# Float32 matmuls for three of four frame blocks: one up pass ahead for the last block, two blocks down dense, two sparse

## What is computed

```python
def block(args):
    xk, ek, gk = args                       # 128 frames; 128 expert numbers and gates per frame
    a = jnp.einsum('nd,ned->ne', xk, u_emb[ek])
    coef = jax.nn.gelu(a, approximate=False) * gk
    return jnp.einsum('ne,ned->nd', coef, v_emb[ek])
```

## Time and profile before

| | |
|---|---|
| median of 3 runs | 1831.16 us (1828.79 to 1844.94) |
| span of the profiled execution | 1734.2 us |
| PE busy | 1694.7 us, 98% |
| DVE busy | 1105.1 us, 64% |
| ACT busy | 577.1 us, 33% |
| POOL busy | 927.0 us, 53% |
| DMA | 351.04 MB, mean 202 GB/s |
| granted TensorE clock | 0.998 |

### The profile page before, as it was taken

The page is one execution under the profiler, slowest core; times in us unless marked ns, Lnnn a source line. Parts: engine busy times, 40 slices in busy tenths (PEclk is TensorE's granted clock), DMA queues, the critical chain, the costliest instruction groups (busy, mean ns, idle before and its releaser), DMA issues.

```text
span 1734.2 us, 23540 instructions
## 1 busy us (share of the span) xinstructions
PE 1694.7 (98%) x7845; PEld 1396.2 (81%) x7845; DVE 1105.1 (64%) x2968; ACT 577.1 (33%) x929; POOL 927.0 (53%) x859
## 2 busy tenths in 40 slices
PE   7999999989999999999999999999999999999997
PEld 6877877778888878888888888888888888888886
DVE  4249968445788864444444444444688888888886
ACT  4333225343322322222222222223333333333333
POOL 3644400003354007777777777771777777777710
PEclk9999999999999999999999999999999999999999
DMA  5322231126667645444447544555999999999991
GB/s 162 105 61 58 65 65 55 42 73 219 214 236 255 218 134 145 146 145 145 145 144 244 146 146 146 146 146 165 385 390 376 370 375 361 373 375 362 378 331 49
DMA packets 182674, 351.04 MB, mean 202 GB/s; under 512 B 35600, under 2 KB 118928, under 8 KB 182448
## 3 DMA queue, kind: packets, MB, share of 16 engines
q1 hardware_dynamic: 147776, 282.74, 49.2%
q0 software_dynamic: 34816, 67.41, 10.8%
HBM read 289.04 MB, written 61.02 MB: 202 GB/s over the span
## 4 chain that ended last, share of the span: by engine, by line
PE 63%; DVE 0%; issue 0%; DVEq 0%; ACT 0%
PE psum L404 21%; PE psum L403 21%; PE psum L405 21%; DVE mixed L2095 0%; DVE mixed L2072 0%; DVEq L2019 0%; DVE rstd_final L815 0%; DVE rstd_final L821 0%; DVE rstd_final L817 0%; DVE rstd_final L819 0%; DVE rstd_final L813 0%; ACT rstd_final L2206 0%; DVE rstd_final L2081 0%; DVE rstd_final L2079 0%
## 5 line engine op out<-in xcount | busy, mean ns | idle before, releaser
L2281 POOL DMA_INDIRECT gate_map<-gate_total,gate_at x384 | 403.5, 1051 | 203.8 <-DVE same_expert L2026 113.2
L403 PE MATMUL psum<-x_hi,ts_hi_u 128*128 128x512 f32 x1024 | 399.1, 390 | 4.0 <-PEq L1641 2.3
L404 PE MATMUL psum<-x_lo,ts_hi_u 128*128 128x512 f32 x1024 | 398.4, 389 | 0.0
L405 PE MATMUL psum<-x_hi,ts_lo_u 128*128 128x512 f32 x1024 | 398.4, 389 | 0.0
L1529 DVE TENSOR_TENSOR ts_lo_u<-ts_raw_u,ts_hi_u 128x1024 fp32r<-128x1024 f32 x116 | 142.3, 1226 | 339.5 <-ACT ts_hi_u L1524 336.8
L403 PE MATMUL psum<-v_hi,c_hi 128*128 128x512 f32 x768 | 298.8, 389 | 0.0
L404 PE MATMUL psum<-v_lo,c_hi 128*128 128x512 f32 x768 | 298.8, 389 | 0.0
L405 PE MATMUL psum<-v_hi,c_lo 128*128 128x512 f32 x768 | 298.8, 389 | 0.0
L1560 ACT ACTIVATE ut_out_u<-psum 128x512 f32<-128x512 f32 x128 | 76.5, 598 | 494.1 <-PE psum L405 494.1
L2186 ACT ACTIVATE v_hi<-v_raw 128x1024 fp32r<-128x1024 f32 x128 | 135.8, 1061 | 312.4 <-PE psum L405 312.4
L2269 POOL DMA_INDIRECT sparse_rows<-in_peer_v,v_row x128 | 164.8, 1288 | 123.2 <-DVE sparse_more L2062 34.5
(11 more groups left out here) (251 smaller groups left out, 2307.5 us busy)
## 6 DMA issues: line engine op xcount, KB each, us to landing
ts_raw_u<-in_peer_u SPq DMA_DIRECT2D x128, 512.0 KB
v_raw<-in_peer_v SPq DMA_DIRECT2D x128, 512.0 KB, 6.1
gate_map<-zeros SPq DMA_DIRECT2D x32, 768.0 KB, 6.5
up_acts<-ut_out_u SPq DMA_DIRECT2D x128, 192.0 KB, 1.9
act_in<-up_acts SPq DMA_DIRECT2D x128, 192.0 KB, 6.3
gate_in<-gate_map SPq DMA_DIRECT2D x128, 192.0 KB, 6.8
raw_in<-in_w_in SPq DMA_DIRECT2D x56, 256.0 KB, 2.8
ts_raw_wq<-in_peer_wq SPq DMA_DIRECT2D x16, 512.0 KB, 6.6
```

Source lines behind the costliest of these rows:

```text
L403: nc.tensor.matmul(out, l_hi, r_hi, start=first, stop=False)
L404: nc.tensor.matmul(out, l_hi, r_lo, start=False, stop=False)
L405: return nc.tensor.matmul(out, l_lo, r_hi, start=False, stop=last)
L2281: nc.gpsimd.indirect_dma_start(gate_cells, bass.IndirectOffsetOnAxis(places["gate_at"][:, b, j:j + 1], 0), dn.total[:, b, j:j + 1], None). ...
```

## The change

Only two blocks remain dense (`DENSE_BLOCKS = NB - 2`). Block 3 becomes the *early* block and block 2 the *late* one; both are summed slot by slot (`SparseSum`).

- **Early pass.** When `route` has ended, PE multiplies the other 104 up tiles with block 3 alone, in plain float32 without a split: 26 groups of 4 tiles, with x of the block (`early_x`, `x_hi` plus `x_lo`, added by DVE at the end of `route`) as the weights and 512 columns of tiles as the moving side, 8 matmuls a group. SP loads 2 MB a group in a ring of three; ACT takes the gelu, SP stores to `up_acts_early`.
- **Up.** The 104 tiles are then done by three passes with 384 columns (`UP_FRAMES`) instead of 512.
- **Rows of the early block.** POOL first scatters the gates of blocks 0 and 1 (256), with no wait for up tiles between them, and then gathers rows and activations for block 3. DVE adds 96 of the rows beside up tiles 40 to 103 of `experts` (`FIRST_ADD`, `UP_ADDS`) and the other 32 beside down tiles 0 to 19 (`LEFT_BY`).
- **Down.** `product` writes `coef` (128 x 256) and PE multiplies it with v in plain float32, 4 matmuls a tile. The splits of v and coef are gone. v is loaded in pairs of tiles into a ring of 20, of which 12 lie in the space of the early tiles and 8 in that of `x_hi` and `x_lo`, which comes free after up. Gate and activation lie beside each other in one map and are loaded as one (`map_in`). Up to four coefficients lead.
- **Rows of the late block.** Gathers for block 2 start once up is done and those of block 3 are through. DVE adds the 128 rows beside down tiles 26 to 123 (`FIRST_LATE`, `late_by`).
- **End.** Block 3 is finished in down, at tiles 20 to 22, block 2 behind the last additions.

The core of the diff:

```diff
-DENSE_BLOCKS = NB - 1
+DENSE_BLOCKS = NB - 2
+LATE_BLOCK, EARLY_BLOCK = NB - 2, NB - 1
+UP_FRAMES = FRAMES - P
+GROUP = 4
+GROUPS = (NKEYS - ROUTE_TILES) // GROUP
...
+class EarlyTiles:
+    RING = 3
...
+    def product(self, nc, pe, g):
...
+        if g >= 2:
+            pe.wait_ge(self.bank_read, g - 1)
+        pe.wait_ge(self.loaded[g % self.RING], 16 * (g // self.RING + 1))
+        for k in range(KT):
+            last = nc.tensor.matmul(self.bank[g % 2], self.x[:, k], self.tiles(g)[:, :, k], start=k == 0, stop=k == KT - 1)
+        last.then_inc(self.product_done, 1)
...
+            dve.wait_ge(wq.product_done, SETS)
+            nc.vector.tensor_tensor(early.x[:], x_hi[:, :, UP_FRAMES:FRAMES].bitcast(F32), x_lo[:, :, UP_FRAMES:FRAMES].bitcast(F32),
+                                    ALU.add).then_inc(early.x_done, 1)
...
+class SparseSum:
+    RING = 8
+    BODY = 8
...
+    def gather_row(self, nc, pool, places, v_rows, j):
+        r = j % self.RING
+        if j >= self.RING:
+            pool.wait_ge(self.row_added, j - self.RING + 1)
...
+    FIRST_ADD, UP_ADDS = 40, 96
+    LEFT_BY = 20
+    FIRST_LATE = 26
...
+    def early_by(n):
+        return max(0, n - FIRST_ADD) * UP_ADDS // (TILES - FIRST_ADD)
+    def early_left_by(e):
+        return UP_ADDS + min(SLOTS - UP_ADDS, e * (SLOTS - UP_ADDS) // LEFT_BY)
+    def late_by(e):
+        return min(SLOTS, max(0, e - FIRST_LATE) * SLOTS // (NKEYS - FIRST_LATE - LAST))
...
+                if e >= COEFS:
+                    dve.wait_ge(down_done, e - COEFS + 1)
+                nc.vector.tensor_tensor(dn.coef[:, e % COEFS], dn.map_in[:, i, 0], dn.map_in[:, i, 1], ALU.mult).then_inc(coef_done, 1)
...
+            soon.zero_more(nc, dve)
+            for m in range(DENSE_BLOCKS * SLOTS):
+                total_gate(m, *place(m))
             for n in range(TILES):
                 if n + 2 < TILES:
                     ut.split_lo(nc.vector, dve, n + (R + 2))
-                for m in range(n * PER_TILE, min((n + 1) * PER_TILE, DENSE_BLOCKS * SLOTS)):
-                    total_gate(m, *place(m))
-            for e in range(EARLY):
+                for j in range(early_by(n), early_by(n + 1)):
+                    soon.add_row(nc, dve, acc, gates, j)
+            for e in range(COEFS):
                 product(e)
...
+            for e in range(NKEYS):
+                if e >= COEFS:
+                    product(e)
+                for j in range(early_left_by(e), early_left_by(e + 1)):
+                    soon.add_row(nc, dve, acc, gates, j)
...
+                for j in range(late_by(e), late_by(e + 1)):
+                    late.add_row(nc, dve, acc, gates, j)
...
+                return nc.tensor.matmul(psum[:, n, :], dn.coef[:, e % COEFS, b * P:(b + 1) * P],
+                                        dn.v(e)[:, half * 512:half * 512 + 512], start=first, stop=final)
...
+            def gather_all(some, cells):
+                for j in range(some.BODY):
+                    some.gather_act(nc, places, cells, j)
+                for j in range(some.RING // 2, some.RING):
+                    some.gather_row(nc, pool, places, v_rows, j)
+                for j in range(some.BODY, 2 * some.BODY):
+                    some.gather_act(nc, places, cells, j)
+                for j in range(some.RING, SLOTS):
+                    some.gather_row(nc, pool, places, v_rows, j)
+                    if j + some.BODY < SLOTS:
+                        some.gather_act(nc, places, cells, j + some.BODY)
             pool.wait_ge(zeroed, 16 * ZERO_STORES)
             for m in range(DENSE_BLOCKS * SLOTS):
-                if m % PER_TILE == 0:
-                    pool.wait_ge(ut.product_done, R + m // PER_TILE)
...
+            gather_all(soon, early_d)
             pool.wait_ge(ut.product_done, NKEYS)
...
+            gather_all(late, late_cells)
```

More of the change, by code:

```diff
@@ L1577, in route @@
+def route(c, x_hi, x_lo, places, expert, gates, zeroed, wq, ut, early, before_start, nc, io, sem, sb, psum, ident, iota, map_d, late_d, early_d, **_):
     G = 4
@@ L1669, in _ @@
                     store_zeros(x)
+            sp.wait_ge(wq.product_done, SETS)
+            for g in range(2):
+                early.load(sp, io["peer_u"], g)
             for t in range(sel_up, ROUTE_TILES):
@@ L2134, in _, with down_bank @@
         def _(pe):
-            def down_bank(i, n, first, final):
+            def down_bank(e, n, first, final):
                 b, half = divmod(n, 2)
-                cols, dcols = slice(b * P, (b + 1) * P), slice(half * 512, half * 512 + 512)
-                return three_pass(nc, psum[:, n, :], dn.c_hi[:, i, cols], dn.c_lo[:, i, cols],
-                                  dn.v_hi[:, i, dcols], dn.v_lo[:, i, dcols], first, final)
-            def down(e, i, first):
-                pe.wait_ge(c_lo_done, e + 1)
+                return nc.tensor.matmul(psum[:, n, :], dn.coef[:, e % COEFS, b * P:(b + 1) * P],
+                                        dn.v(e)[:, half * 512:half * 512 + 512], start=first, stop=final)
@@ L2144, in down, with wait_tile @@
+            def wait_tile(e):
+                if e % 2 == 0:
+                    pe.wait_ge(v_in[e % V_RING // 2], 16 * (e // V_RING + 1))
+                pe.wait_ge(coef_done, e + 1)
+            def down(e):
+                wait_tile(e)
                 for n in range(OUTS):
-                    last = down_bank(i, n, first, False)
+                    last = down_bank(e, n, e == 0, False)
                 last.then_inc(down_done, 1)
             def last_tiles(b):
-                for i in range(RING):
+                for e in range(NKEYS - LAST, NKEYS):
@@ L2151, in last_tiles @@
                     if b == 0:
-                        pe.wait_ge(c_lo_done, NKEYS - RING + i + 1)
+                        wait_tile(e)
                     for n in (2 * b, 2 * b + 1):
-                        last = down_bank(i, n, False, i == RING - 1)
-                        if i == RING - 1:
+                        last = down_bank(e, n, False, e == NKEYS - 1)
+                        if e == NKEYS - 1:
                             last.then_inc(bank_done, 1)
+            for g in range(GROUPS):
+                early.product(nc, pe, g)
@@ L2158, in _ @@
+            up_hi, up_lo = x_hi[:, :, 0:UP_FRAMES], x_lo[:, :, 0:UP_FRAMES]
             with pe.Fori(0, TILES // 2) as it:
                 for par in range(2):
-                    ut.product(nc, pe, x_hi, x_lo, it * 2 + (R + par), par, False)
-            for i in range(RING):
-                down(i, i, i == 0)
-            with pe.Fori(1, NKEYS // RING - 1) as it:
-                for i in range(RING):
-                    down(it * RING + i, i, False)
+                    ut.product(nc, pe, up_hi, up_lo, it * 2 + (R + par), par, False, ut.bank[par][:, 0:UP_FRAMES])
@@ L2166, in _ @@
+            for e in range(NKEYS - LAST):
+                down(e)
             for b in range(DENSE_BLOCKS):
@@ L2202, in _ @@
                     act.wait_ge(acc_done, 2 * n + half + 1)
-                    nc.scalar.activation(dn.rows[:, n, dcols], acc[:, b, dcols], ACT.Square,
+                    nc.scalar.activation(dn.early_rows[:, n, dcols], acc[:, b, dcols], ACT.Square,
                                          accum_out=ss[:, b, half:half + 1]).then_inc(squared, 1)
```

409 lines of the change are left out of this document (227 added, 182 removed).

## The result

| | before | after |
|---|---|---|
| median of 4 runs | 1830.39 us (1828.79 to 1844.94) | 2061.65 us (2057.53 to 2064.09) |
| ratio after / before | | 1.1242, 95% interval 1.1194 to 1.1291 |
| span of the profiled execution | 1734.2 us | 2055.7 us |

The change makes the kernel 12% slower. The sign is as forecast, the size is not: 1867 us were predicted, with 1905 as the upper end. The four runs of the kernel after took 1.8 us more than their spans; the median of the kernel before stands 96 us above the one span that was profiled.

The account below looks back on a forecast made before the run. PE was taken as the present bound, POOL and DMA second. PE alone gave −37.9 us (1696 us), but POOL's chain of gathers made the span 1769.6 us; with the 97.0 us gap 1867 us, range 1797 to 1905.

Parts of the forecast that it names:

- 97 us: Whole run: gap between profiled span 1734.2 and median 1831.2 us, added unchanged to the forecast span to give 1867 us.
- the forecast's sum: Whole span: POOL's chain of scatters and gathers ends late, giving 1769.6 against 1734.2 us, +35.4 us.
- Rival (d): Early pass or later: scatters wait for landing, or gathers and v loads saturate the DMA; span above 1820 us, chance 0.10.
- pitch of a row in the up stage: Up stage: POOL's time for one row and one activation gather of block 3, taken as 3.1 us.
- pitch of a late row: Down stage: POOL's time for one row and one activation gather, taken as 2.95 us.
- zero of 0 to 2: Barrier at 636 us: block 3's address arithmetic and x_hi plus x_lo on DVE cost 0 to 2 us, summed as 0.
- half a hold per instruction: POOL's gathers: each 1.28 us DVE addition holds one POOL instruction 0.64 us on average, less 0.12 us.
- the sign that I had named: Up stage from tile 40: PE below 100% and `ts_lo_u` late behind `early_rows` would show the forecast right.
- POOL's chain of rows: Up into down: block 3's rows 8 to 95 at 3.1 us let down start at 1289 instead of 1248 us.
- POOL without idle time except issue: From 640 us to the last gather: POOL never idles except its 0.30 us issue gaps, a sign the forecast is right.
- rival (b): A draw, including the DMA as bound in down (449 against PE's 439 us): span 1716 to 1752 us, chance 0.20.
- The Trainium skill's rule that I had weighed: SBUF: two-input DVE instructions and GpSimd instructions reading SBUF exclude each other; the second waits, 1.34 against 0.96 us in the trace.

Follow-up runs that it names:

- c4: Kernel after with POOL waiting once for all 256 gate totals, then scattering without waits; on a disturbed chip, 2102.1 us.
- g1: Kernel after, unedited, run again on a quiet chip: 1771.92 us, span 1770.1, beside a kernel before of 1741.2 us.
- e7: Kernel after without the early pass's plain loads after its third group: span 2054.3 us, beside a kernel before of 1834.04 us.
- e8: Kernel after with scatters paced by PE's products, and without block 2's 128 activation gathers: span 1843.3 us, beside a kernel before of 1834.04 us.
- e5: Kernel after with POOL waiting for DVE's gate totals once per 16 scatters instead of before each: span 2046.2 us.
- c1: Kernel after, unedited, run again on a disturbed chip: 2071.5 us, beside a kernel before of 1845.25 us.
- c3: Kernel after with scatters paced, 5 per early group then 3 per up tile, on a disturbed chip: 1893.9 us.
- the paced one: Kernel after with scatters waiting for PE's products, 5 per early group, then 3 per up tile: 1786.0 us quiet, 1893.9 us disturbed.
- c2: Kernel before, unedited, run again with its own trace on a disturbed chip: 1857.7 us.

## Why the prediction was right and wrong

**The step that failed** is the sentence "The profiled span and the median of the runs lie 97.0 us apart (1831.2 − 1734.2), which I leave as they are: 1867 us." I treated 97 us as something fixed around the span. In every run that had both numbers, device time and span differ by 1.8 to 2.2 us. The 97 us were late increments in the up stage, of the kind that c4 ties to POOL's stream, and the change makes that stream denser and takes its pace away. In the kernel before POOL waits for the up tile's product ahead of every fourth scatter, so a delay of that very increment stops POOL too; in the changed kernel nothing in POOL's scatters waits for PE, and they go on past the gaps (256 in 358 us, against 343 in g1). Cost: from about 97 to 286 us (2055.7 − 1770.1). With the 97 us carried over as a constant, 1867 us could not hold it. That the median is slower, as forecast, is mostly luck: of its 231 us about 31 are those of the forecast's sum (1771.9 − 1741.2 in g1), the rest is a loss that the forecast did not have. Rival (d), "worse", got 0.10 and a mechanism about bandwidth and landing, which is not what happened; e7 excludes it for the early pass.

**The sum itself came out** where it could be seen alone, in g1, but not for its reasons in the up stage:

| step | forecast | g1 |
|---|---|---|
| early pass | 178.3 us | 178.2 |
| last scatter issued | 977 us | 986.6 |
| row 8 of block 3 | 1010 us | 1020.0 |
| pitch of a row in the up stage | 3.1 us | 2.85 (rows 8 to 96) |
| down starts | 1289 us | 1283.3 |
| pitch of a late row | 2.95 us | 2.96 (rows 8 to 112) |
| last gather | 1737 us | 1733.1 |
| end of the last matmul | 1760 us | 1761.0 |
| span | 1769.6 us | 1770.1 |

The close end hides errors that cancel. The scatters were 10 us late: they began at 643.8 us, not 640, and the first 48 took 1.37 us each beside DVE's totals, which I had priced at 1.26. PE left the barrier at 640.4 us, not 636.5: 2.9 us waiting for the sum of `x_hi` and `x_lo`, which I had put at zero of 0 to 2:

```profile
PEld psum L1623 <- DVE early_x L1982: 2.9, 1, 2.9
```

The rows of the up stage went the other way, 22 us better: from row 40 on they come 2.77 us apart, exactly PE's 1.5 per 4.16 us, with POOL issuing without idle time. My average of half a hold per instruction was too dear; why, no run here separates. And from 1098 us to the end of the stage PE never stood:

```profile
1100.00:1250.00 150.00, 150.00 (x867) 150.00 (x866) 110.00 (x97) 52.15 (x73) 116.87 (x109) 1.00 1.00 365
```

So the sign that I had named, PE below 100% from tile 40 on and `ts_lo_u` late behind `early_rows`, is there only at the first rows: PE loses about 11 us near 1010 us, where DVE waits 12.2 us for the first activations (forecast: 5 to 8). The start of down was to be the end of POOL's chain of rows; it was the end of PE's own work, 433 us and 32 us of stops. That 1283 lies near 1289 is luck.

Missed altogether were the other 19 or so of these 32 us: halfway through the up stage SP issues six loads of 1 MB for v, and the loads of the coming up tiles stand behind them. SP's issues in g1 in that stretch and after it:

```profile
1061.03 3.04 SPq L1534 DMA_DIRECT2D ts_raw_u<-in_peer_u  x1
...
1083.51 0.41 SPq L1534 DMA_DIRECT2D ts_raw_u<-in_peer_u  x1
```

PE stops four times between 1054.9 and 1083.6 us, 14.8 us in all from start to start, and its matmuls stand 0.32 us apart instead of 0.17 for a while behind them; in the kernel after 1328.6 to 1339.5 us is the same place. It moved the start of down but hardly the end: POOL, whose stream sets the end, waited for additions only 3.1 us in all.

**"POOL without idle time except issue"** from the first scatter to the last gather is confirmed by g1. What ended waits in its down stage (us, times, longest):

```profile
DVE coef L2172 <- DMA map_in<-gate_act_map: 61.5, 26, 5.4
DVE mixed L2098 <- DMA late_rows<-in_peer_v,v_row: 54.4, 36, 2.5
...
POOL late_rows L2070 <- issue: 39.0, 128, 0.3
POOL late_act L2075 <- issue: 39.0, 128, 0.3
```

In down PE does wait for `coef`, and POOL's chain gave the end. But POOL is not the only bound there. In e8 half of its instructions of the stage were gone; window and waits of e8:

```profile
1450.00:1800.00 350.00, 343.68 (x793) 149.33 (x794) 197.51 (x255) 1.54 (x5) 141.03 (x121) 1.00 1.02 405
...
DVE coef L2177 <- DMA map_in<-gate_act_map: 152.6, 69, 5.0
POOL late_rows L2070 <- DVE late_more L2103: 107.2, 39, 17.9
```

POOL now waits for additions and DVE for the maps, at 405 GB/s and a share of 1.02, and down still took 474 us, not the 439 to 450 that I had expected. The total mixes two parts. Tiles 0 to 25, ahead of the late rows, took 116 us against 107 in the three kernels beside it on that chip (e5 to e7); from tile 26 on e8 took 358 us, those three 367 to 369, g1 369, and PE alone would take 350. So POOL's missing instructions were worth about 10 of 19 us, and about 8 remain. These I put down to the DMA, rival (b), by the waits and the 405 GB/s; no run takes DMA traffic away there. Disturbed chips disturb down as well (483, 486 and 492 us in c1, c4 and c3), so that e8 can be held only against its neighbours. The Trainium skill's rule that I had weighed ("SBUF — State Buffer", section "Who interferes with whom") stays supported by the 1.37 us beside the totals.

**In what sense slower.** On a quiet chip the change costs 1771.9 / 1741.2, 1.8% in single runs, as the spans of the forecast said (1769.6 / 1734.2, 2.0%); on a disturbed one 12.3% (2071.5 / 1845.3), the median 12.4%. It is slower on both. No version here beats the kernel before: the paced one is 2.7% slower on a quiet chip and 2.6% on a disturbed one (1893.9 / 1845.3; 1.9% against the 1857.7 us of c2), where it takes back 178 us of the change's 226.

**Not shown.** Whether short pauses of POOL are enough or its wait for PE's own increment is needed, which I only argue (the paced early pass took 183.5 us in c3 and 180 in e8); what the pace alone is worth in the kernel before on a disturbed chip; and whether scatters do more harm than gathers: both do some, as 1404 us in the kernel after shows for gathers. Since each chip was used in one group of runs only, its state at that time cannot be told from the chip itself. Why one does it and another not, and why 44.80 us, I cannot say.

## What to carry to other kernels

Before a sum is made against a profile, put its span beside the times: where they differ by more than a few us, something happens in the timed runs that this profile doesn't show, and it has to be found and priced, not carried along. Compare kernels, and above all experiments, only with the kernel before from the same chip; four clean runs on a quiet chip could decide nothing here and led to a wrong theory all the same. A wait that looks redundant because it is nearly always met may be what stops an engine in time; if POOL's indirect DMAs are to be set free of the product's pace, look at a profile from a chip where increments come late.

## What the runs showed of the hardware

- On two of the five chips of the experiments, while POOL issues indirect DMAs one behind the other (0.96 us and 0.30 us between), semaphore increments of PE reached ACT and SP up to 38 us after the matmul's end, both in the same instant, and DVE's totals, which wait for DVE's own increments, stood up to 3.5 us apart instead of 0.27. With scatters alone one increment of PE came per 44.80 us (c4). On the three other chips, beside the same streams, no recorded update of an engine's semaphore stands more than 0.02 us behind its instruction.
- It needs no plain DMA traffic (5 GB/s in e7) and no work on DVE (c4); no run has both away. The Trainium skill, "DMA: Bandwidth & Descriptors", section "Anatomy of one DMA — SWDGE (gpsimd) path", puts a DMA's semaphore update at about 100 ns once the receipt is there; an engine's increment here took up to 38 us.
- The trace names such a release "remote" or "another core or an unknown queue" on a kernel of one core. Two engines released in the same 0.01 us by a third that had long been done is the sign.
- The gaps cost more than their length: after 38 us without work (792.57 us of c4) the first six distances between PE's records were 0.85 to 1.02 us, twice the usual 0.43, and the granted clock between 700 and 760 us of e7 was 0.59, close to the lower of its two levels (1.2 of 2.4 GHz).
- Behind six loads of 1 MB SP's own issues took 3.0 us each instead of 0.4 (g1, 1061 to 1070 us).
